# Memory keys and values: four-byte products replaced by three single-pass products of split operands

## The reference, cut to what matters

```python
mem_n = rms_norm_2(mem, norm_mem_kv[l])          # (1, 256, 1024)
k, v = jnp.split(mem_n @ w_kv, 2, axis=-1)       # w_kv: (1024, 2048)
```

## Time and profile before

| | us |
|---|---|
| median of 3 runs | 1781.56 |
| lowest and highest | 1779.45, 1783.88 |
| profiled execution, span from first to last instruction | 1781.0 |
| profiled execution, own time | shown only as its span |
| mean granted TensorE clock | 0.994 of 2.4 GHz |
| TensorE busy | 1730.8 |
| VectorE, ScalarE, GpSimd busy | 951.6, 698.4, 205.1 |

### The profile page before, as it was taken

How to read it: one execution, slowest core, us unless ns; L and a number is a source line. 1 busy time by engine, 2 the same in 40 slices (tenths; PEclk the granted TensorE clock), 3 DMA queues, 4 the chain that set the end, 5 groups by cost and what they waited for, 6 DMA issues and landing times.

```text
span 1781.0 us, 20994 instructions
## 1 busy us (share of the span) xinstructions
PE 1730.8 (97%) x8107; PEld 1371.6 (77%) x8107; DVE 951.6 (53%) x1709; ACT 698.4 (39%) x1267; POOL 205.1 (12%) x168
## 2 busy tenths in 40 slices
PE   8989999999999999999999999999999999999998
PEld 5558788667888888877788787775887888887887
DVE  4455566444463333357555777665544655556334
ACT  3233344744333322344464555542333422223234
POOL 3242100002000000020000333320200200000000
PEclk9999999999999999999999999999999999999999
DMA  6243202132433323323221111113220232222221
GB/s 193 75 134 95 95 25 74 52 111 73 127 95 96 99 92 105 104 73 106 72 68 52 36 60 36 60 57 141 92 90 24 86 102 96 95 95 95 95 95 48
DMA packets 122372, 152.24 MB, mean 85 GB/s; under 512 B 8827, under 2 KB 110609, under 8 KB 121762
## 3 DMA queue, kind: packets, MB, share of 16 engines
q1 hardware_dynamic: 119986, 140.19, 24.4%
q0 software_dynamic: 2288, 10.71, 1.7%
HBM read 144.90 MB, written 6.00 MB: 85 GB/s over the span
## 4 chain that ended last, share of the span: by engine, by line
PE 90%; DVE 5%; ACT 2%; issue 1%; DMA 1%; POOL 0%; DVEq 0%; ACTq 0%; POOLq 0%
PE bank L1981 50%; PE bank L2015 16%; PE bank L1261 2%; PE bank L1679 2%; PE bank L2237 2%; PE bank L2356 2%; PE bank L2234 1%; PE bank L1212 1%; PE bank L2329 1%; PE bank L774 1%; PE bank L1124 1%; PE bank L1129 1%; PE bank L1713 1%; PE bank L2112 1%; PE bank L2040 1%
## 5 line engine op out<-in xcount | busy, mean ns | idle before, releaser
L1981 PE MATMUL bank<-act_high,w_high 128*128 128x512 f32 x1360 | 552.1, 406 | 8.5 <-DVE act_low L965 2.6
L1981 PE MATMUL bank<-act_high,w_low 128*128 128x512 f32 x1360 | 532.2, 391 | 0.0
L1981 PE MATMUL bank<-act_low,w_high 128*128 128x512 f32 x1360 | 531.2, 391 | 0.0
L643 ACT ACTIVATE w_high<-ring 128x1024 fp32r<-128x1024 f32 x222 | 234.3, 1056 | 672.2 <-PE bank L1981 458.4
L667 DVE TENSOR_TENSOR w_low<-ring,w_high 128x1024 fp32r<-128x1024 f32 x202 | 257.2, 1274 | 220.4 <-ACT w_high L643 220.4
L1981 PEld LDWEIGHTS bank<-act_high,w_high 128*128 128x128 f32 x1360 | 256.2, 188 | 70.2 <-issue 14.6
L1981 PEld LDWEIGHTS bank<-act_high,w_low 128*128 128x128 f32 x1360 | 256.0, 188 | 55.3
L1981 PEld LDWEIGHTS bank<-act_low,w_high 128*128 128x128 f32 x1360 | 256.4, 189 | 51.8 <-issue 4.4
L2015 PE MATMUL bank<-act_high,w_high 128*128 128x512 f32 x416 | 162.1, 390 | 2.3 <-DVE arena L3263 1.2
L2015 PE MATMUL bank<-act_high,w_low 128*128 128x512 f32 x416 | 161.9, 389 | 0.0
L2015 PE MATMUL bank<-act_low,w_high 128*128 128x512 f32 x416 | 161.9, 389 | 0.0
(11 more groups left out here) (372 smaller groups left out, 2230.3 us busy)
## 6 DMA issues: line engine op xcount, KB each, us to landing
ring<-in_ffn_w SPq DMA_DIRECT2D x32, 1024.0 KB, 5.3
ring<-in_w_in SPq DMA_DIRECT2D x28, 1024.0 KB, 5.1
ring<-in_w_up SPq DMA_DIRECT2D x22, 1024.0 KB, 5.0
ring<-in_w_down SPq DMA_DIRECT2D x11, 1024.0 KB, 4.8
ring<-in_w_mem_kv SPq DMA_DIRECT2D x8, 1024.0 KB, 5.3
ring<-in_cmp_w SPq DMA_DIRECT2D x4, 1024.0 KB, 7.8
ring<-in_w_out SPq DMA_DIRECT2D x4, 1024.0 KB, 5.6
ring<-in_w_mix_out SPq DMA_DIRECT2D x4, 1024.0 KB, 5.2
```

The lines of the kernel that those rows point to most:

```text
L643: nc.scalar.activation(part(w_high, name), raw_part(name), ACT.Copy).then_inc(w_rounded, 1)
L1981: last = nc.tensor.matmul(b[0:rows, :], w[:, k, 0:rows], a, start=k == 0 and n == 0, stop=k == KT - 1 and n == 2)
```

## The change

The eight key tiles and four value tiles become split products. Sixteen weight parts of 128x1024 are added between those of `s_v` and of the output projection `wo`: `memk0` to `memk7`, and `memv0a`, `memv0b` to `memv3b` (a value tile's 256 columns in two halves of the contraction). ScalarE rounds them, in `take_mem_k` and between the stick-breaking heads; GpSimd writes the remainders. The normalised memory is split as well: eight copies of 128x256 on ScalarE, eight subtractions on VectorE, in units 9 to 12. `mem_t` moves to the first half of its buffer, the parts take the second half. The ring slots of `mkv0` to `mkv7` come free at the remainder and not at the product. Each pair of products on TensorE, four records before, becomes six single-pass products of 256 columns.

```diff
@@ w_parts
+            split(f"memk{m}", f"mkv{m // 2}", (m % 2) * P)
+        for i in range(4):
+            for half in range(2):
+                split(f"memv{i}{'ab'[half]}", f"mkv{4 + i}", half * PART, 256,
+                      f"memv{i}" if half else ("mem", i + 1))
@@ round_weights
+                    if isinstance(last, tuple):
+                        eng.wait_ge(mem_used, last[1])
@@ mem_t, mem_parts
-            return nt_high[:, 2 * D + 256 * k:2 * D + 256 * (k + 1)]
+            return nt_high[:, 256 * k:256 * (k + 1)]
+        def mem_parts(k):
+            return act_high[:, 2 * D + 256 * k:2 * D + 256 * (k + 1)], act_low[:, 2 * D + 256 * k:2 * D + 256 * (k + 1)]
@@ gpsimd
-            split_weights(eng, "s_v1")
+            split_weights(eng, "memv0a")
             taken(eng, "memk7")
             eng.dma_start(mem_k_dram, mem_k1).then_inc(mem_k_stored, 16)
             for h in range(4):
+                split_weights(eng, f"memv{h + 1}a" if h < 3 else "memv3b")
                 taken(eng, f"memv{h}")
@@ tensor, mem_pair
                     if u == 0:
-                        eng.wait_ge(mem_normed, 8)
+                        eng.wait_ge(mem_rest, 8)
+                if is_key:
+                    if k0 == 0:
+                        eng.wait_ge(w_split, w_part_at[name] + 1)
+                    w_h, w_l = part(w_high, name), part(w_low, name)
+                    for k in (k0, k0 + 1):
+                        a_h, a_l = mem_parts(k)
+                        for n, (w, a) in enumerate(((w_h, a_h), (w_h, a_l), (w_l, a_h))):
+                            ins = nc.tensor.matmul(b[:, 0:256], w[:, k, :], a, start=k == 0 and n == 0,
+                                                   stop=k == KT - 1 and n == 2)
...
+                if piece % 4 == 0:
+                    eng.wait_ge(w_split, w_part_at[part_name] + 1)
+                    for n, (a, w) in enumerate(((a_h, w_h), (a_h, w_l), (a_l, w_h))):
+                        ins = nc.tensor.matmul(b[:, t * 256:(t + 1) * 256], a, w[:, at * 256:(at + 1) * 256],
+                if piece == 3:
+                    ins.then_inc(mem_used, 1)
@@ scalar, take_mem_k
                     take(f"memk{m}", mem_k1[:, 256 * m:256 * (m + 1)], w=256)
+                    round_weights(eng, f"memk{m + 2}" if m < 6 else f"memv0{'ab'[m - 6]}")
+                if u in range(9, 13):
+                    for k in (2 * u - 18, 2 * u - 17):
+                        eng.wait_ge(mem_normed, k + 1)
+                        nc.scalar.activation(mem_parts(k)[0], mem_t(k), ACT.Copy).then_inc(mem_rounded, 1)
+                if u in (11, 12):
+                    round_weights(eng, f"memk{u - 11}")
@@ scalar, stick-breaking heads
+                if h + 1 < 4:
+                    round_weights(eng, f"memv{h + 1}a")
                 stick_exps(eng, h)
+                if h + 1 < 4:
+                    round_weights(eng, f"memv{h + 1}b")
@@ vector, normalise_memory
+                if u in range(9, 13):
+                    for k in (2 * u - 18, 2 * u - 17):
+                        eng.wait_ge(mem_rounded, k + 1)
+                        high, low = mem_parts(k)
+                        nc.vector.tensor_tensor(low, mem_t(k), high.bitcast(F32), ALU.subtract).then_inc(mem_rest, 1)
```

More of the change, by code:

```diff
@@ L523, in two_blocks @@
         for m in range(8):
+            split(f"memk{m}", f"mkv{m // 2}", (m % 2) * P)
[3 more added lines that the diff above has]
+                      f"memv{i}" if half else ("mem", i + 1))
+        for m in range(8):
             split(f"wo{m}", f"out{m // 2}", (m % 2) * P)
@@ L612, in raw_part @@
                 return slot(load_name)[:, c0:c0 + D].rearrange("p (k c) -> p k c", c=P)
+            if cols == 256:
+                return slot(load_name)[:, c0:c0 + PART].rearrange("p (k c) -> p k c", c=P)
             return slot(load_name).rearrange("p (k c) -> p k c", c=256)[:, :, c0:c0 + cols]
@@ L638, in round_weights @@
                     last = w_parts[w_part_at[in_pairs[pair_at[name] - PAIRS]]][3]
-                    if isinstance(last, int):
+                    if isinstance(last, tuple):
+                        eng.wait_ge(mem_used, last[1])
+                    elif isinstance(last, int):
                         eng.wait_ge(hidden_used, last)
@@ L1752, in two_blocks @@
         mem_normed = sem("mem_normed")
+        mem_rounded = sem("mem_rounded")
+        mem_rest = sem("mem_rest")
+        mem_used = sem("mem_used")
         mem_k_stored = sem("mem_k_stored")
@@ L2226, in mem_pair @@
                         eng.wait_ge(sb_zs, TT)
-                    slot_ready(eng, load_name)
                     if u == 0:
-                        eng.wait_ge(mem_normed, 8)
[L2230 to L2238, removed]
@@ L2239, in mem_pair @@
-                if u % (4 if is_key else 8) == (3 if is_key else 7):
+                        eng.wait_ge(mem_rest, 8)
+                b = bank[bank_at[name]]
+                if is_key:
[7 more added lines that the diff above has]
+                                                   stop=k == KT - 1 and n == 2)
+                    if k0 == 6:
+                        ins.then_inc(tile_filled, 1)
+                    return
@@ new lines, in mem_pair @@
+                piece = u % 8
+                half, t = piece // 4, piece // 2 % 2
+                part_name = f"{name}{'ab'[half]}"
+                if piece % 4 == 0:
+                    eng.wait_ge(w_split, w_part_at[part_name] + 1)
+                w_h, w_l = (part(x, part_name).rearrange("p k c -> p (k c)") for x in (w_high, w_low))
+                for at in (2 * (piece % 2), 2 * (piece % 2) + 1):
+                    a_h, a_l = (a[:, t * P:(t + 1) * P] for a in mem_parts(4 * half + at))
+                    for n, (a, w) in enumerate(((a_h, w_h), (a_h, w_l), (a_l, w_h))):
+                        ins = nc.tensor.matmul(b[:, t * 256:(t + 1) * 256], a, w[:, at * 256:(at + 1) * 256],
+                                               start=(piece, at, n) == (0, 0, 0),
+                                               stop=piece == 7 and (at, n) == (3, 2))
@@ L2240, in mem_pair @@
+                if piece == 3:
+                    ins.then_inc(mem_used, 1)
+                if piece == 7:
                     ins.then_inc(tile_filled, 1)
@@ L2962, in normalise_memory @@
                         .then_inc(taken_dve, 1)
[L2963 to L2967, removed]
+                if u in range(8, 12):
+                    for k in (2 * u - 16, 2 * u - 15):
+                        nc.vector.scalar_tensor_tensor(mem_t(k), mem_raw(k), col("nmkv", k), mem_rb, ALU.mult,
+                                                       ALU.mult).then_inc(mem_normed, 1)
+                if u in range(9, 13):
[3 more added lines that the diff above has]
+                        nc.vector.tensor_tensor(low, mem_t(k), high.bitcast(F32), ALU.subtract).then_inc(mem_rest, 1)
             attend_dve_early(eng, 0, N_B1, normalise_memory)
```

## The result

The changed kernel takes 1803.34 us (median of 4 runs, 1798.16 to 1805.72) against 1781.4 us before: ratio 1.0112, interval 1.0089 to 1.0135. By the medians it is 21.9 us slower, by the ratio 20.0 (15.9 to 24.0); 13.2 us were forecast. The sign and the mechanism were right, the size was not.

A forecast was written before the change was run, and what follows sets the result against it. TensorE bounds the kernel (97% busy), except a VectorE-ScalarE chain just before the first key product. -8.5 + 10.6 + 7.9 + 3.2 = +13.2 us on 1781.0, plus 0.56 around the span: about 1795 us, range 1781 to 1806.

The forecast's parts named there:

- Products, -8.5 us: TensorE's memory products: six single-pass steps of 0.12 us replace four records of 0.862 us, net -8.5 us.
- the 0.6 I gave back: TensorE: 0.6 us taken off the 9.1 us product saving for steps from one kind of product to the other.
- narrow product isn't cheap: Rival on TensorE: at 0.15 us a step the products save nothing, 1806 us; at 0.227, 1836; chance 0.1.
- faster: Rival: products at 0.107 us save 13.6 us, start costs only 5 us, remainders free; 1773 us; chance 0.1.
- the hold doesn't bite: Rival: GpSimd's remainders fall into VectorE's gaps, only chain and ScalarE roundings cost; +0.1, 1782 us; chance 0.19.
- Start, +10.6 us: Before the first key product: longer chain plus two normalises held by GpSimd remainders, 10.6 us, bounds 7 to 13.
- the chain term: Units 9 to 13: ring of exponentials, normalise, shift, gains, roundings and weights delays the first key product by 7.3 us.
- Eight spots in the loop, +7.9 us: Attention unit loop: GpSimd remainders after key tiles hold VectorE's normalise, delaying TensorE's transpose; 7.9 us, bounds 2 to 10.
- The rounding on ScalarE costs nothing: Loop spots: ScalarE's rounding fits in 0.66 us free there, the rest under GpSimd's hold; no cost of its own.
- Heads, +3.2 us: Stick-breaking heads: GpSimd remainders of first value parts hold VectorE's mask additions; 3.2 us, bounds 0 to 5.
- The clock: Rival: longer waits at 222 to 240 us lower TensorE's clock, up to 3 us, in the range; no chance given.
- The hold itself: VectorE's SBUF-to-SBUF operation stands until GpSimd is nearly done, about 0.2 us before its record ends.

The follow-up runs named there:

- e1: Kernel before with only the six single-pass products in place of the four-byte ones, no rounding or remainder; 1771.85 us, ratio 0.9953.
- e2: Changed kernel with GpSimd's 16 memory remainders 8 columns wide instead of 1024, every wait kept; 1784.93 us, ratio 1.0012.
- e5: Kernel before plus 16 GpSimd subtractions (128x1024) whose results nothing uses, where the changed kernel has its remainders; 1794.83 us, ratio 1.0065.
- e4: Changed kernel with the roundings and remainders of the memory's activation parts one unit later (units 10 to 13); 1802.58 us, ratio 1.0125.
- e6: Changed kernel with each GpSimd memory weight remainder cut into four instructions of 256 columns, same work and engine; 1790.74 us, ratio 1.0049.
- e3: Changed kernel with the 16 memory weight remainders on VectorE instead of GpSimd, one unit later; 1787.21 us, ratio 1.0038.
- e7: e3 with the activation parts of the first units also one unit later; 1784.85 us, ratio 1.0018.
- e9: e2 (narrow remainders) with the activation parts of the first units also one unit later; 1782.25 us, ratio 1.0003.
- e8: Only value tiles split, against the kernel before; activation parts rounded in units 20 to 48, value remainders on VectorE; 1775.38 us, ratio 0.9968.

## Why the prediction was right and where it was off

- **Products, -8.5 us: right.** The forecast step of 0.12 us was measured as 0.119, and e1 saves 9.5 us. The 1 us is the 0.6 I gave back for changes between kinds of product, and the step. The rival "narrow product isn't cheap" falls with it, "faster" with the time itself, and "the hold doesn't bite" with e2 and e5. Not foreseen: in the stages the keys' share isn't won in full (e1: 2.8 us in start and loop).
- **Start, +10.6 us: the stage grew by 10.6 us, 10.9 against e1.** The first key product started at 239.33 us (forecast: about 240). Of this the chain with its follow-up is 7.9 us (e2 minus e1; forecast 7.3) and the remainders 3.0 (forecast 3.3). But the chain term as forecast held no clock. From the transpose of unit 13 to that of unit 14 TensorE works without a wait, for 3.19 us against 1.54 in e1, and up to unit 16 for 3.46 against 2.93: some 2.2 us are the lower clock. In e2 these two stretches are 3.20 and 3.45 us, so the 2.2 are part of the 7.9, and the chain itself gave some 5.7 where 7.3 were forecast. The match is partly luck.
- **Eight spots in the loop, +7.9 us: mis-sized.** After minus e2 is 10.1 us for units 19 to 58, 1.26 us a spot instead of 0.99, and another 1.7 us (e2 minus e1) stay with narrow remainders. "The rounding on ScalarE costs nothing" doesn't hold as it stands; whether the 1.7 us are the roundings or the waits for the parts was not tried apart. The first spot itself was well read: 0.79 us of idle TensorE at 252.72 where I worked out 1.0.
- **Heads, +3.2 us: the total right**, 3.1 (after minus e2), its parts not. The forecast adds up four heads with such a part (1.1, 0.75, 0.75, 0.6); the program has three. The mask additions at 359.22, 377.56 and 398.03 are held, as the forecast said of the one at 336.37, for 2.25, 2.48 and 1.10 us; TensorE waits for 1.04 us behind the first and 0.58 behind the second, and for none behind the third. One more wait, of 0.67 us at 408.46, comes behind a second part: a scaling of VectorE (L806) takes 3.35 us from 401.72, beside the remainder of 402.06, and VectorE comes late to the next mask addition.
- **The clock: the step that failed.** I put it into the range, as a rival of up to 3 us, and not into the sum. There are two falls, over about 17 us at the start and 7 us from 332 to 339. In units 58 to 63 there is no remainder; the two kernels with the second fall there (the change and e4) take 15.7 us, all others 12.5: 3.2 us. (e6 shows a short one just behind, and its next stage is 1.2 us longer.) In the 3.4 us before this fall TensorE was busy for 2.09 us, with waits behind the last of the ten remainders; in the same place before and e2 have 2.84 and no fall. With the 2.2 at the start that is 5.4 us, brought on by the waits and paid after them. The second fall rests on two traces, one execution each; whether every execution has it is open.
- **The sum.** By its own terms against what was measured: -8.5 became -9.5, 10.6 became 10.9, 7.9 became 11.8, 3.2 became 2.9, and 3.2 for units 58 to 63 was missing: 19.3 in place of 13.2. With the 7.5 us that the stages show for the products in place of 9.5 it is 21.3, the ledger's sum; the rest to the 21.9 of the medians is within what differs from run to run.
- **The hold itself.** A free normalise of 31 columns takes 0.30 us; the held one ended at 232.85, so its 0.30 us would have begun at 232.55, 0.27 us before the remainder's record ends at 232.82; at 236.47 and 250.83 the same reckoning (0.35 and 0.48 us) gives 0.27 too. I had read 0.2. But this figure goes with the kind of the held step and not with its width: it is 0.26 to 0.27 for all eight held normalises that multiply by two scalars (line 1209), of 31 to 512 columns, 0.20 for the two that multiply by one (line 1211, 316.79 and 326.97), and 0.15 for the three mask additions. So the reckoning takes in something of the held step itself, and no run shows that the hold ends before the remainder does. By the Trainium skill, "SBUF — State Buffer", section "SBUF: two separate sides", the loser is blocked for the whole instruction: the runs agree as to the instruction being the unit of the hold (e6), and do not settle the last quarter of a microsecond.

## What to carry to other kernels

An idle engine is not a free one: before work goes to GpSimd, look in the trace for what VectorE does in the same microseconds, and count one hold for each of its wide SBUF-to-SBUF steps that the added instruction will meet; if it must be GpSimd, cut the instruction into pieces, and if a short step on VectorE does the same, that can be cheaper. Apply a cheaper product only where its preparation fits: here half of the change (the values), prepared where the engines had room, won 5.9 us, while the whole, prepared in a hurry before the first key product and beside GpSimd, lost 21.9. Where new waits lower the clock, add what the lower clock takes from the work behind them.

## What the runs showed of the hardware that was not expected

- A clock fall costs after its cause. With the waits up to 226.6 us the granted clock of the changed kernel fell to 0.50 for some 17 us, and a product step took 0.21 us in place of 0.119. e2, e3, e4, e6, e7 and e9 also show a stretch below 1.0 between 226 and 244 us, and so does e5, which has only the holds; before, e1 and e8 show none.
- The hold doesn't take every VectorE step. In e5, inside one subtraction (318.58 to 320.93), the shift that reads a bank takes 0.42 us, the copy out of a bank 0.68 and the one-column reciprocal 0.16, as long as without one; the normalise of 256 columns at 319.89 takes 1.19 in place of 0.35. In the changed kernel the subtraction of a suffix sum, with one of its two inputs in a bank, takes 0.55 us at 397.44 inside a remainder, as without one, and the mask addition behind it, with both inputs in SBUF, 1.10 in place of 0.29. So steps that read a bank went through, and wide steps from SBUF to SBUF were held; the one-column steps went through although they too read and write SBUF, and why is open.
